# A hybrid encoder block on one core: small mixer products in row and column groups, two-pass suffix sums, and another order of work at expert 0

## The reference, cut to what matters

```python
log_a = log_sigmoid(gate_low @ w_gate_up + b_gate) / GLA_TAU     # (512, 16) @ (16, 512)
cum   = cumsum(log_a over each chunk of 64 tokens)
total = cum[:, :, -1]                                            # one row a chunk
k_dec = k * exp(total - cum)        # the suffix sum after each token
state = exp(total) * state + k_dec^T v                           # chunk by chunk
```

## Time and profile before

| | |
|---|---|
| median of 3 runs | 1784.98 us (1784.5 to 1785.11) |
| profiled execution, its own time | 1784.43 us |
| its span, first to last instruction | 1782.8 us |
| mean granted TensorE clock | 0.991 |
| DVE busy | 1342.0 us (75%), 1172 instructions |
| ACT busy | 1106.2 us (62%), 930 instructions |
| POOL busy | 296.6 us (17%) |
| DMA | 487.87 MB, mean 274 GB/s |

### The profile page before, as it was taken

The page is one execution under the profiler, slowest core; times in us unless marked ns, Lnnn a source line. Parts: engine busy times, 40 slices in busy tenths (PEclk is TensorE's granted clock), DMA queues, the critical chain, the costliest instruction groups (busy, mean ns, idle before and its releaser), DMA issues. The chain is left out here.

```text
span 1782.8 us, 23461 instructions
## 1 busy us (share of the span) xinstructions
PE 1735.6 (97%) x8295; PEld 1413.4 (79%) x8296; DVE 1342.0 (75%) x1172; ACT 1106.2 (62%) x930; POOL 296.6 (17%) x227
## 2 busy tenths in 40 slices
PE   6999999999999999999999999999999999999995
PEld 5787788888887777888878888888888888888884
DVE  6214414433446799999899999999999999999998
ACT  3525324464323467777677777777777777777775
POOL 3000000000001065222211212121221212121211
PEclk9999999999999999999999999999999999999997
DMA  7322232122323489999999999999999999999994
GB/s 260 97 93 72 71 94 72 48 72 72 112 92 131 177 313 354 386 379 381 377 378 377 369 370 388 366 369 383 381 375 367 386 373 377 373 390 362 370 378 163
DMA packets 115594, 487.87 MB, mean 274 GB/s; under 512 B 18861, under 2 KB 49581, under 8 KB 66395
## 3 DMA queue, kind: packets, MB, share of 16 engines
q1 hardware_dynamic: 99474, 455.66, 66.5%
q0 software_dynamic: 16064, 31.55, 6.4%
q10 hardware_dynamic: 8, 0.01, 0.0%
HBM read 476.12 MB, written 28.36 MB: 283 GB/s over the span
## 5 line engine op out<-in xcount | busy, mean ns | idle before, releaser
L1355 DVE TENSOR_TENSOR wlo<-raw,whi 128x2048 fp32r<-128x2048 f32 x382 | 863.4, 2287 | 65.9 <-ACT whi L946 64.6
L946 ACT CAST whi<-raw 128x2048 fp32r<-128x2048 f32 x382 | 724.7, 1913 | 198.8 <-PE psA L1610 164.6
L1608 PE MATMUL psA<-whi,xT_hi 128*128 128x512 f32 x1036 | 406.9, 393 | 1.9 <-issue 1.3
L1610 PE MATMUL psA<-whi,xT_lo 128*128 128x512 f32 x1036 | 403.3, 389 | 0.0
L1609 PE MATMUL psA<-wlo,xT_hi 128*128 128x512 f32 x1036 | 403.3, 389 | 0.0
L1608 PEld LDWEIGHTS psA<-whi,xT_hi 128*128 128x128 f32 x1036 | 194.6, 188 | 43.4 <-issue 4.2
L1610 PEld LDWEIGHTS psA<-whi,xT_lo 128*128 128x128 f32 x1036 | 194.5, 188 | 40.7
L1609 PEld LDWEIGHTS psA<-wlo,xT_hi 128*128 128x128 f32 x1036 | 194.6, 188 | 39.0
L1608 PE MATMUL psX<-whi,aT_hi 128*128 128x512 f32 x496 | 195.8, 395 | 0.0
L1610 PE MATMUL psX<-whi,aT_lo 128*128 128x512 f32 x496 | 193.5, 390 | 0.0
L1609 PE MATMUL psX<-wlo,aT_hi 128*128 128x512 f32 x496 | 193.3, 390 | 0.0
(11 more groups left out here) (362 smaller groups left out, 2031.7 us busy)
## 6 DMA issues: line engine op xcount, KB each, us to landing
raw<-in_w_gate_up SPq DMA_DIRECT2D x254, 1024.0 KB, 8.9
raw<-in_w_down SPq DMA_DIRECT2D x128, 1024.0 KB, 8.2
raw<-in_w_in SPq DMA_DIRECT2D x32, 1024.0 KB, 5.4
raw<-in_w_gla_proj SPq DMA_DIRECT2D x4, 1024.0 KB, 5.1
raw<-in_w_fox_proj SPq DMA_DIRECT2D x4, 1024.0 KB, 5.2
raw<-in_w_out SPq DMA_DIRECT2D x4, 1024.0 KB, 5.1
xt<-in_x SPq DMA_DIRECT2D x4, 512.0 KB, 6.1
h_dram<-xt POOLq DMA_DIRECT2D x4, 512.0 KB, 5.3
```

Of the source, the lines that this page charges most:

```text
L946: s_.copy(xsplit(c)[0], xraw(slot)).then_inc(hi_ready, 1)
L1355: v.tensor_tensor(lo, xraw(slot), hi.bitcast(F32), ALU.subtract).then_inc(lo_ready, 1)
L1608: mm(dst, sh, mh, start=first, stop=False)
L1610: return mm(dst, sl, mh, start=False, stop=last)
```

## The change

In the mixers:

- `smT` becomes 128 rows: the 24 rows of token tile t lie at partitions 32t, next to a row of ones. `w_up` and the gate's bias are loaded four times, at partitions 0, 32, 64, 96. The products of s = 4 and s = 5 for tile t use rows 32t to 32t+31 only, and the four of s = 4 write four PSUM banks.
- `la` is split into `la_hi` (ACT, hook 6) and `la_lo` (DVE, hook 6); the suffix sums are two fp32r products each and move to s = 8, 9.
- The totals at s = 10 are four products with a 128x32 selector as stationary operand and 512 columns moving, into partitions 32t of one bank; ACT takes exp of 128x512, PE transposes the four head blocks at s = 11, ACT copies `decay`.
- DVE adds up the forget tiles before F (`lsf_sum`), so a tile needs one product with `ones` at most.

At the tail: `mix_norm` starts its first normalising instruction before the root is waited for; ACT takes `logits_out(2)` before `std`; PE takes `turn_logits(2)` and `pick(1)` before `turn_h2(3, .)`, and `pick(2)` before `positions(3)`; DVE takes `list_row(1)` and `tile_lo` of tile 2 behind `xT_lo`.

```diff
@@ SP, load_params
-            sp.dma_start(w_up[0:RANK, :], a["w_gla_gate_up"][0]).then_inc(params_in, 16)
-            sp.dma_start(w_up[32:33, :], a["b_gla_gate"]).then_inc(params_in, 16)
+            for r in range(TT):
+                sp.dma_start(w_up[32 * r:32 * r + RANK, :], a["w_gla_gate_up"][0]).then_inc(params_in, 16)
+                sp.dma_start(w_up[32 * r + RANK + FH:32 * r + RANK + FH + 1, :], a["b_gla_gate"]).then_inc(params_in, 16)
@@ ACT, hook
-                s_.copy(smT[0:RANK + FH, :], psX[0:RANK + FH, 2, :]).then_inc(smT_evac, 1)
+                for r in range(TT):
+                    rows = slice(32 * r, 32 * r + RANK + FH)
+                    ins = s_.copy(smT[rows, :], psX[0:RANK + FH, 2, r * P:(r + 1) * P])
+                ins.then_inc(smT_evac, 1)
...
+            if s == 6:
+                act.wait_ge(la_ready, 1)
+                s_.copy(la_hi[:], la[:]).then_inc(la_ready, 1)
...
-            if s == 9:
+            if s == 10:
                 act.wait_ge(tot_done, 1)
-                s_.activation(decay, psX[:, 0, 0:GH * NCH]..., ACT.Exp, scale=1.0 / TAU)
+                s_.activation(totals[:], psX[:, 0, :], ACT.Exp, scale=1.0 / TAU).then_inc(dec_ready, 1)
+            if s == 11:
+                act.wait_ge(tot_done, 2)
+                s_.copy(decay..., psX[:, 1, :]...[:, :, 0:2]).then_inc(dec_ready, 1)
@@ DVE, hook
+            if s == 6:
+                dve.wait_ge(la_ready, 2)
+                v.tensor_tensor(la_lo[:], la[:], la_hi[:].bitcast(F32), ALU.subtract).then_inc(la_ready, 1)
...
+                seq.link(v.tensor_tensor(lsf_sum[:, 0, :], lsf[:, 0, :], lsf[:, 1, :], ALU.add))
+                v.tensor_tensor(lsf_sum[:, 1, :], lsf_sum[:, 0, :], lsf[:, 2, :], ALU.add).then_inc(lsf_ready, 1)
@@ PE, hook
             if s == 5:
                 for t in range(TT):
-                    ins = mm(psX[:, t, :], smT[:, t * P:(t + 1) * P], w_up[:], start=True, stop=True)
+                    rows = slice(32 * t, 32 * (t + 1))
+                    ins = mm(psX[:, t, :], smT[rows, :], w_up[rows, :], start=True, stop=True)
-            if s in (7, 8):
-                pe.wait_ge(la_ready, 1)
-                    mm(psX[:, t, :], suffix[:], la[:, t, :], start=True, stop=True).then_inc(suf_done, 1)
-            if s == 9:
+            if s in (8, 9):
+                pe.wait_ge(la_ready, 3)
+                    mm(psX[:, t, :], suffix[:], la_hi[:, t, :], start=True, stop=False)
+                    mm(psX[:, t, :], suffix[:], la_lo[:, t, :], start=False, stop=True).then_inc(suf_done, 1)
+            if s == 10:
                 pe.wait_ge(kd_mul, TT)
+                for t in range(TT):
+                    ins = mm(psX[32 * t:32 * (t + 1), 0, :], chunk_sel[:], la[:, t, :], start=True, stop=True)
+            if s == 11:
+                pe.wait_ge(dec_ready, 1)
                 for h in range(GH):
-                    for t in range(TT):
-                        ins = mm(psX[:, 0, o:o + 2], la[:, t, h * GDK:(h + 1) * GDK], chunk_sel, ...)
+                    ins = nc.tensor.transpose(psX[:, 1, h * P:(h + 1) * P], totals[:, h * P:(h + 1) * P], ident[:])
@@ DVE, mix_norm
-            dve.wait_ge(std_ready, TT + t + 1)
-            seq.link(v.reciprocal(rstd[:, t:t + 1], rstd[:, t:t + 1]))
+            dve.wait_ge(var_ready, TT + t + 1)
             for half in range(2):
-                seq.link(v.scalar_tensor_tensor(row, row, mv[:, t, 0:1], lnmix_g[:, cols], ...))
+                seq.mark(v.scalar_tensor_tensor(row, row, mv[:, t, 0:1], lnmix_g[:, cols], ...))
+                if half == 0:
+                    dve.wait_ge(std_ready, TT + t + 1)
+                    seq.mark(v.reciprocal(rstd[:, t:t + 1], rstd[:, t:t + 1]))
+                seq.join()
@@ DVE, after the last mix_norm
-        list_row(1)
...
-        tile_lo(2, 2, 2)
         dve.wait_ge(early_done, 1)
...
         (xT_lo)
+        tile_lo(2, 2, 2)
         tile_lo(3, 3, 3)
+        list_row(1)
         seq.mark(weigh(3))
@@ PE, after the w_out products
         pick(0)
+        turn_logits(TT - 2)
+        pick(1)
         turn_h2(TT - 1, 0)
-        turn_logits(TT - 2)
         turn_h2(TT - 1, 1)
         route(TT - 1)
         positions(2)
         turn_logits(TT - 1)
-        pick(1)
+        pick(2)
         positions(3)
-        pick(2)
         pick(3)
```

More of the change, by code:

```diff
@@ L154, in build @@
     gtmp = at("gtmp", 168, [P, 2, T])
-    smT = at("smT", 172, [33, T])
-    w_up = at("w_up", 174, [33, T])
+    smT = at("smT", 172, [P, P])
+    w_up = at("w_up", 174, [P, T])
+    la_hi = at("la_hi", 136, [P, TT, GH * GDK], F32R)
+    la_lo = at("la_lo", 144, [P, TT, GH * GDK], F32R)
+    totals = at("totals", 184, [P, GH * GDK])
+    chunk_sel = at("chunk_sel", 188, [P, 32])
     ln_rows = at("ln_rows", 160, [97, 512])
@@ L223, in build @@
     ident = at("ident", 192, [P, P])
-    suffix = at("suffix", 192.5, [P, P])
+    suffix = at("suffix", 192.5, [P, P], F32R)
     incl = at("incl", 193, [P, P])
@@ L260, in build @@
     lst = vec(TT, FH)
+    lsf_sum = lst[:, 0:2, :]
     b_f = vec(FH)
     g_norm = vec(2)
-    chunk_sel = vec(2)
     smax, snmax, ssum, srec = vec(2), vec(2), vec(2), vec(2)
@@ L556, in _ @@
         marks = Steps(pool, const_ready, 0)
-        for t, v in ((ident, 0.0), (ident_b, 0.0), (suffix, 1.0), (incl, 1.0), (strict, 1.0),
+        for t, v in ((ident, 0.0), (ident_b, 0.0), (incl, 1.0), (strict, 1.0),
                      (negmask, 0.0), (smT, 1.0)):
             marks.mark(g.memset(t[:], v))
-        for t in (ones_r, sel):
+        for t in (ones_r, sel, suffix):
             marks.mark(g.memset(t[:].bitcast(F32), 1.0))
-        marks.link(g.memset(chunk_sel, 0.0))
+        marks.link(g.memset(chunk_sel[:], 0.0))
         for b in range(3):
@@ L574, in _ @@
         sel_of(ident[:], [[-1, P]], ALU.not_equal, 1.0, 0, 1)
-        sel_of(suffix[:], [[-1, P]], ALU.is_gt, 0.0, 0, 1)
+        marks.mark(g.affine_select(out=suffix[:], in_=suffix[:].bitcast(F32), pattern=[[-1, P]], compare_op=ALU.is_gt, fill=0.0,
+                                   base=0, channel_multiplier=1))
         sel_of(incl[:], [[1, P]], ALU.is_ge, 0.0, 0, -1)
@@ L586, in _ @@
         marks.join()
-        marks.link(g.memset(suffix[CHUNK:P, 0:CHUNK], 0.0))
+        marks.link(g.memset(suffix[CHUNK:P, 0:CHUNK].bitcast(F32), 0.0))
         marks.link(g.memset(chunk_sel[0:CHUNK, 0:1], 1.0))
@@ L861, in hook @@
                     s_.activation(gtmp[:, b, :], psX[:, t, :], ACT.Exp, scale=1.0 / TAU).then_inc(kd_exp, 1)
-            if s == 9:
+            if s == 10:
                 act.wait_ge(tot_done, 1)
-                s_.activation(decay, psX[:, 0, 0:GH * NCH].rearrange("p (h n) -> p h n", h=GH), ACT.Exp,
-                              scale=1.0 / TAU).then_inc(dec_ready, 1)
+                s_.activation(totals[:], psX[:, 0, :], ACT.Exp, scale=1.0 / TAU).then_inc(dec_ready, 1)
+            if s == 11:
+                act.wait_ge(tot_done, 2)
+                s_.copy(decay.rearrange("p h (t j) -> p (h t) j", j=2),
+                        psX[:, 1, :].rearrange("p (g c) -> p g c", c=32)[:, :, 0:2]).then_inc(dec_ready, 1)
             if s == 10:
@@ L1697, in hook @@
                 for t in range(TT):
-                    ins = mm(psX[:, 3, t * FH:(t + 1) * FH], smT[0:RANK + FH, t * P:(t + 1) * P],
-                             ident[0:RANK + FH, RANK:RANK + FH], start=True, stop=True)
+                    rows = slice(32 * t, 32 * t + RANK + FH)
+                    ins = mm(psX[:, t, 0:FH], smT[rows, :], ident[rows, 32 * t + RANK:32 * t + RANK + FH],
+                             start=True, stop=True)
                 ins.then_inc(fl_done, 1)
@@ L1747, in hook @@
             if s == FSLOT:
-                pe.wait_ge(lsf_ready, 1)
+                pe.wait_ge(lsf_ready, 2)
                 pe.wait_ge(gla_out, GH)
+                ahead = (None, lsf[:, 0, :], lsf_sum[:, 0, :], lsf_sum[:, 1, :])
                 for t in range(TT):
-                    for u in range(t + 1):
-                        tri = incl if u == t else ones
-                        mm(psX[:, 0, t * FH:(t + 1) * FH], tri[:], lsf[:, u, :], start=u == 0, stop=u == t)
+                    dst = psX[:, 0, t * FH:(t + 1) * FH]
+                    if t >= 1:
+                        mm(dst, ones[:], ahead[t], start=True, stop=False)
+                    mm(dst, incl[:], lsf[:, t, :], start=t == 0, stop=True)
                 for t in range(TT):
-                    for u in range(t + 1):
-                        tri = incl if u == t else ones
+                    if t >= 1:
                         for r in range(2):
-                            ins = mm(psX[32 * r:32 * r + FH, 1, t * P:(t + 1) * P], lsf[:, u, :], tri[:],
-                                     start=u == 0, stop=u == t)
+                            mm(psX[32 * r:32 * r + FH, 1, t * P:(t + 1) * P], ahead[t], ones[:], start=True, stop=False)
+                    for r in range(2):
```

(2 more changed lines are left out.)

31 lines of the change are left out of this document (17 added, 14 removed).

## The result

Faster: 1770.88 us median of 6 runs (1769.05 to 1771.71) against 1784.74 (1783.72 to 1785.11, 6 runs); ratio 0.9923, 95% interval 0.9913 to 0.9933. That is 13.9 us; 13.2 were forecast. The profiled execution took 1769.05 us, the shortest of the six, with a span of 1767.5: 15.3 less than before, 1.4 more than the medians differ.

What follows compares the result with a forecast made beforehand. PE sets the pace (busy 1058.56 of 1080 us in the experts), DVE close behind. Projections 10.9 plus expert 0 2.3 make 13.2 us saved, from the median 1784.98 to 1771.8 us; range 1768.5 to 1776.5.

Steps and rivals of the forecast that it cites:

- Gate, row groups: Projections, s = 5: gate products side by side in four row groups, 1.29 instead of 5.37 us; 4.1 us saved.
- Forget columns: Projections, s = 4: four products in four row groups and banks, 0.7 left of 1.21 us; 0.5 saved.
- Suffix sums: Projections, s = 8, 9: fp32r products at 0.91 us instead of f32 at 1.77, twice; 1.7 us saved.
- Forget sum: Projections, s = 30: 14 and 28 records instead of 20 and 40, through `lsf_sum`; 1.35 us saved.
- Totals: Projections, s = 10, 11: column groups 1.29 plus transposes 0.66 instead of 5.23 us; 3.3 saved, at best 3.6.
- The log-decay chain: Gate to `la_lo` before hook 8: 15.5 us against PE's 16.3, 0.8 cover, no stall; 0 to 1.5 possible.
- rival 2: Log-decay chain late at hook 8 and expert 0 gives nothing: 8.4 us saved, 1776.6; chance 0.12.
- rival 4: SP's queue at the start: six added DMAs delay `bias_raw`, 24 us net slower, 1809; chance 0.04.
- rival 1: Groups don't run side by side, or the mode change costs what they save: 4.6 us left, 1780.4; chance 0.05.
- The tail: Picks to expert 1: `first_tile` 4.6 us sooner, DVE gives back 1.6; 3.0 left, 1.3 at low clock, 2.3 taken.
- Rival 3: Expert 0 gives all of 4.6, clock stays and clamp doesn't hold PE: 15.5 us saved, 1769.5; chance 0.15.
- The loop of the experts: Long stretch of the experts: only starts sooner; the prediction is wrong if it takes back what it was handed.

Runs made afterwards that it cites:

- gate_128_rows: Kernel before with the gate's two operand tiles made 128 rows high instead of 33, ones and zeros in the added rows; 1783.05 us, ratio 0.9994.
- totals_one_group: Changed kernel with the four totals products all in array columns 0 to 31, each into its own bank, instead of four column groups; 1773.02 us, ratio 0.9932.
- changed_again: The changed kernel itself, timed and profiled a second time; 1770.65 us, ratio 0.9934.
- tail_only: Kernel before with only the new order at the tail and at expert 0, no mixer edit; 1781.47 us, ratio 0.9985.
- suffix_f32: Changed kernel with the suffix sums as unsplit f32 products of `la` again, at the new slots; 1772.33 us, ratio 0.9931.
- dve_order_only: Changed kernel with PE's order of picks and ACT's late `logits_out` put back as before, DVE's new tail order kept; 1773.23 us, ratio 0.9936.
- counts_on_act: Changed kernel with the three copies of `member` made by ACT instead of DVE; 1770.42 us, ratio 0.9925.
- pe_order_only: Changed kernel with DVE's tail order put back as before, PE's order of picks and ACT's early `logits_out` kept; 1774.96 us.
- mixers_only: Changed kernel with the order at the tail and at expert 0 put back as before, all mixer edits kept; 1774.21 us, ratio 0.9946.
- list_late: Changed kernel with DVE's `list_row(1)` moved behind the clamp of expert 0 and POOL's list writes behind its gather; 1770.52 us, ratio 0.9927.

## Why the prediction held, step by step

- **Gate, row groups**: 4.1 forecast, 4.15 measured. The price read off the experts' bias product (1.29) came out as 1.22. The part put down to the clock (1.7) is 1.9, by gate_128_rows.
- **Forget columns** 0.5: 0.63. **Suffix sums** 1.7: 1.63. **Forget sum** 1.35: 1.33.
- **Totals** 3.3: 3.65, just past the bound of 3.6. Column groups cost 1.14, a little less than the row groups they were priced by, and the four transposes 0.44. I had taken 0.66 for them, the duration of a row that ran at full clock too; its next start came after 0.49. The slow stretch went, as I said, but my ground for it was wrong: I put it down to the full width of the array, and in totals_one_group, with a quarter of the width, it is gone as well.
- **The log-decay chain** had 1.1 us of cover, 0.8 were forecast: no stall, and rival 2, which needed one, is out. **SP's queue** (rival 4): six DMAs at 0.3 us. The groups overlap (rival 1): both kinds measured.
- **The tail**: net 2.75 by clamp 1, forecast 2.3, and that agreement is partly luck: against the 3.0 that I had for a clock that stays, three sizes were off, by -0.4, +0.8 and -0.6. `first_tile` is 4.2 us sooner, 4.6 forecast with the clock up. PE stood 0.44 and 0.67 us before the last two picks for DVE's `slots`; from the start of the choice for tile 3 to its slots DVE took 3.2 us, where my list had 2.8:

```profile
606.60 0.18 DVE L1336 TENSOR_TENSOR logits<-psA,b_rt 128x32 f32<-128x32 f32 x1
...
609.49 0.29 DVE L1365 TENSOR_SCALAR slots<-iota,posm 128x128 fp32r<-128x128 f32 x1
```

  DVE's longer way behind `xT_lo` was to give back 1.6. It gives back 0.8 at clamp 0: from `xT_lo` it takes 25.96 us without idle time, not 26.6. Another 0.6 goes at clamp 1, for which I had nothing: the clock, whose fall I held as likely as not at the picks (3.0 or 1.3, so 2.3), does not fall there but one step later, behind the wait for the clamp that I had priced without it. That costs PE 1.6 us (`turn_a`, the transposes of expert 0's activations, comes at 650.25 against 663.20, 12.95 us sooner where the clamp had come 14.55), but DVE is the bound in that stretch, and only 0.6 arrive at clamp 1. Rival 3 had the clock right at the picks and the clamp wrong, and is 1.4 us too fast. The table product behind `vals_ready` did not wait: it starts 8.57 us behind expert 0's first product, before 8.68.
- **The loop of the experts** took nothing back: the clamp of expert 2 stands 13.94 us sooner, the medians 13.9.

The forecast of 13.2 is low by 0.7. All of that lies in the projections (10.9 forecast, 11.6 measured by distances from hook 4 to the route) and the tail (0.45), less the 0.4 that the start came late. The five measured terms of the projections add up to 11.4; the other 0.2 I can put to no hook.

## What to carry to other kernels

Price a small product by the distance between two hooks, and look at the granted clock behind it: a third of what such a step costs can be in the large products that follow (1.9 of 5.37 us). Before looking for a price elsewhere, look for the same form in the same trace; here the experts' bias product gave the gate's to 0.07 us. Where two engines feed each other through small steps, one engine's new order may gain little or lose without the other's (77.30 and 75.65 to clamp 1 with one, 73.02 with both, against 76.58), and a gain at one point can be gone at the next, so count to where the steady loop begins. A step moved off the critical wait still costs where its engine has no idle time until the next one.

## What the runs showed of the chip that I had not expected

- The clock (2.4 GHz) falls to 1.2 GHz although PE is never idle: behind four f32 products of 33 rows (3.6 us) it does, behind the same four with 128 rows, the added ones zeros in `w_up`, it doesn't. Behind four f32 products that fill 32 of 128 columns (3.7 us) it doesn't; behind 16 that stream two columns each (3.5 us) it does.
- Behind the wait at the start of expert 1 it fell with 1.87 to 1.91 us (changed, changed_again, tail_only, suffix_f32, totals_one_group) and didn't with 1.93 (dve_order_only) or 1.33 (counts_on_act). With 0.95 it fell in pe_order_only and didn't in before, mixers_only and list_late. Which it will be can't be read from the wait alone. Nor can the length: the stretch at half clock there lasted 3.4 us in the changed kernel and nearly 7 in totals_one_group, and at the picks less than 7 in the kernel before and 10 in mixers_only.
- Four f32 products side by side cost 1.22 us in row groups into four banks and 1.14 in column groups into one bank, one after the other 3.5 to 3.7: a factor of 2.8 to 3.2, not 4.
